# Three mixers and a mixture of experts on one core: the recurrence's projections first, the attention values projected in the rotation steps, the recurrence's output gate computed late and read from PSUM

## What is computed

```python
h = x @ w_cols
h_gla, h_rwkv, h_nsa, h_vres = _split(h, ...)
gq, gk, gv, gg, galr = _split(h_gla, GLA_COLS)
rr, rk, rv, rwlr, ralr, rglr = _split(_token_shift_mix(h_rwkv, rwkv_mu[l]), RWKV_COLS)
o_gla, o_rwkv, o_nsa = _gla_mixer(...), _rwkv7_mixer(...), _nsa_mixer(...)
mix = jnp.concatenate([o_gla, o_rwkv, o_nsa], axis=-1) @ w_out[l]
...
g = (jax.nn.sigmoid(g_lr) @ g2).astype(f32)        # in _rwkv7_mixer
return ((y + bonus) * g).astype(dt)
```

## Time and profile before

| | |
|---|---|
| median of 3 runs | 2021.17 us (2020.33 to 2023.05) |
| profiled execution | 2023.03 us, its span 2021.2 us |
| PE busy | 1966.1 us (97%) |
| DVE, ACT, POOL busy | 855.1, 313.4, 45.1 us |
| mean granted PE clock | 0.993 |
| HBM read | 596.73 MB, mean 296 GB/s |

### The profile page before, as it was taken

One profiled execution on the slowest core, in us unless ns is written; L12 is line 12 of the kernel. 1 busy time (PEld: TensorE's weight loads), 2 busy tenths in 40 slices (PEclk: granted clock), 3 DMA queues, 4 the chain that ended last, 5 costly groups with the idle time before them and its releaser, 6 DMA issues.

```text
span 2021.2 us, 24513 instructions
## 1 busy us (share of the span) xinstructions
PE 1966.1 (97%) x9835; PEld 1115.1 (55%) x9835; DVE 855.1 (42%) x1538; ACT 313.4 (16%) x725; POOL 45.1 (2%) x62
## 2 busy tenths in 40 slices
PE   8999999999999999999999999999999999999997
PEld 7878588748777588749553333333333333333332
DVE  1487588865587586754731111111111111111112
ACT  1335211101435111103410000000000000000001
POOL 0021000000021000000000000000000000000000
PEclk9999999999999999999999999999999999999999
DMA  8540067646630165436298999999999999999996
GB/s 332 217 158 1 32 234 308 251 167 278 263 126 1 41 226 199 171 154 266 89 393 373 428 429 429 427 429 429 427 430 427 430 429 427 429 427 430 429 428 287
DMA packets 44275, 598.75 MB, mean 296 GB/s; under 512 B 5056, under 2 KB 5360, under 8 KB 8464
## 3 DMA queue, kind: packets, MB, share of 16 engines
q1 hardware_dynamic: 44208, 597.82, 71.9%
HBM read 596.73 MB, written 1.07 MB: 296 GB/s over the span
## 4 chain that ended last, share of the span: by engine, by line
PE 82%; DMA 15%; DVE 3%; issue 0%; ACT 0%; SPq 0%; DVEq 0%
PE ps L2349 18%; DMA ring<-in_stream 15%; PE ps L1404 12%; PE ps L2397 8%; PE ps L1489 7%; PE ps L402 6%; PE ps L2323 3%; PE ps L1273 3%; PE ps L361 2%; PE ps L2338 2%; PE ps L419 2%; PE ps L2434 2%; PE ps L1820 1%; PE ps L1986 1%; PE ps L1150 1%; PE ps L1167 1%
## 5 line engine op out<-in xcount | busy, mean ns | idle before, releaser
L2349 PE MATMUL ps<-ring,HT 128*64 128x512 f32 x2176 | 479.4, 594 | 20.0 <-DMA ring<-in_stream 19.2
L2349 PEld LDWEIGHTS ps<-ring,HT 128*64 128x64 f32 x2176 | 152.9, 137 | 340.1 <-issue 289.3
L2397 PE MATMUL ps<-SB,HT 128*64 128x512 f32 x1088 | 249.2, 612 | 0.9 <-ACT HT L2460 0.9
L2505 DVE TENSOR_SCALAR HT<-ps 128x512 f32<-128x512 f32 x34 | 23.5, 692 | 449.8 <-PE ps L2349 449.8
L2397 PEld LDWEIGHTS ps<-SB,HT 128*64 128x64 f32 x1088 | 77.0, 140 | 170.2 <-issue 170.2
L1404 PE MATMUL ps<-ring,SB 128*128 128x256 f32 x704 | 156.0, 379 | 0.3 <-DVE SB L331 0.3
L2454 ACT ACTIVATE HT<-HT 128x512 f32<-128x512 f32 x34 | 21.5, 631 | 843.9 <-DVE HT L2505 843.9
L1404 PEld LDWEIGHTS ps<-ring,SB 128*128 128x128 f32 x704 | 133.6, 190 | 18.8 <-issue 0.7
L2517 DVE TENSOR_TENSOR HT<-ps,TOK 128x512 f32<-128x512 f32 x34 | 23.5, 692 | 281.3 <-PE ps L2397 281.3
L402 PE MATMUL ps<-SB,ring 128*128 128x256 f32 x576 | 126.9, 384 | 1.3 <-DMA ring<-in_stream 1.3
L402 PEld LDWEIGHTS ps<-SB,ring 128*128 128x128 f32 x576 | 110.8, 193 | 17.1 <-issue 1.6
(11 more groups left out here) (489 smaller groups left out, 2251.8 us busy)
## 6 DMA issues: line engine op xcount, KB each, us to landing
ring<-in_stream SPq DMA_DIRECT2D x210, 2048.0 KB, 16.6
SB<-in_stream SPq DMA_DIRECT2D x68, 2048.0 KB, 24.8
SB<-in_ln SPq DMA_DIRECT2D x8, 512.0 KB, 7.0
CST<-in_const SPq DMA_DIRECT2D x1, 1362.0 KB, 5.5
PAR<-in_layer SPq DMA_DIRECT2D x2, 558.5 KB, 11.6
X<-in_x SPq DMA_DIRECT2D x1, 1024.0 KB, 4.9
HN<-in_head_norm SPq DMA_DIRECT2D x2, 512.0 KB, 12.8
SB<-in_cond_row SPq DMA_DIRECT2D x2, 512.0 KB, 10.9
```

Of the source, the lines that this page charges most:

```text
L2349: m = pe.matmul(ps[HD * half:HD * (half + 1), a, :], XE[:, 2 * b + k, q * SLOTS_E:(q + 1) * SLOTS_E], w[:, k, a, half, :], start=False, st ...
L2397: m = pe.matmul(ps[HD * c:HD * (c + 1), 3, :], EHT[:, k, HD * b:HD * (b + 1)], w[:, k, c, :], start=b + k == 0, stop=b + k == 4, skip_grou ...
```

## The change

The columns of the weights are laid out anew: the recurrence's channels are groups 0 to 3 and the first half of 4, GLA's queries and keys follow in 5 and 6, and DVE's `mix_dve` waits for five groups in place of seven. The projections are counted anew: group 11 is now the 24 gate columns of both token halves (`project_gates_pe`), 12 and 13 are GLA's values and gate (`project_tokens_pe`), and group 14 the 256 columns of attention values (`project_values_pe`). The values are projected in the rotation steps 2 and 3 in 16 products, where 13 dummy products go; the slot of their weights is released only there. GLA's gate and the low-rank products come after group 8, not 9. The recurrence's output gate is computed in the second chunk, where three dummy products go, and DVE reads it from PSUM; ACT's copy of it goes. POOL's blocks (`cmp_pool`) move from XT's to LW's and AA's memory and wait for `rw_ops`.

```diff
-T_GQ, T_GK, T_R, T_K, T_V, T_WA, T_G1, T_MISC, T_VC, T_KC, ... = 0, 2, 4, 6, 8, 10, 11, 12, 13, 14, ...
+T_R, T_K, T_V, T_WA, T_G1, T_MISC, T_VC, T_GQ, T_GK, T_KC, ... = 0, 2, 4, 6, 7, 8, 9, 10, 12, 14, ...
...
-                return "proj_ready", 15 * l + [2, 4, 6, 8, 10, 13, 15][s]
+                return "proj_ready", 15 * l + [2, 4, 6, 8, 10, 15, 14][s]
...
+        def project_gates_pe(pe, l):
+            w = slot(AT["in", l, 5]).rearrange("p (k n) -> p k n", k=KT)
+            pe.wait_ge(S("proj_evac"), 15 * l + 8)
+            for t in range(NT):
+                for k in range(KT):
+                    m = pe.matmul(ps[:, proj_bank(11), 24 * t:24 * (t + 1)], XT[:, k, t * P:(t + 1) * P], w[:, k, 384:408],
+                                  start=k == 0, stop=k == KT - 1)
+            m.then_inc(S("proj_ready"), 1)
...
+        def project_values_pe(pe, l, t, ks):
+            w = slot(AT["in", l, 5]).rearrange("p (k n) -> p k n", k=KT)
+            for k in ks:
+                m = pe.matmul(ps[:, proj_bank(14), t * 256:(t + 1) * 256], XT[:, k, t * P:(t + 1) * P], w[:, k, P:P + 256],
+                              start=k == 0, stop=k == KT - 1)
+            if t == NT - 1 and ks[-1] == KT - 1:
+                m.then_inc(S("proj_ready"), 1)
...
         def mix_dve(v, l, I, L):
-            v.wait_ge(S("proj_evac"), 15 * l + 7)
+            v.wait_ge(S("proj_evac"), 15 * l + 5)
...
         def rwkv_ranks_pe(pe, l):
...
-            for t in range(NT):
-                pe.matmul(ps[:, 5, t * T:(t + 1) * T], HT[:, T_G1, t * P:(t + 1) * P], par("g2"), start=True, stop=False)
-                m = pe.matmul(ps[:, 5, t * T:(t + 1) * T], HT[0:32, T_MISC, t * P:(t + 1) * P], par("misc")[0:32, :],
-                              start=False, stop=True)
             m.then_inc(S("rw_z"), 1)
+        def rwkv_gate_high_pe(pe, t):
+            pe.matmul(ps[:, 5, t * T:(t + 1) * T], HT[:, T_G1, t * P:(t + 1) * P], par("g2"), start=True, stop=False)
+        def rwkv_gate_low_pe(pe, t):
+            m = pe.matmul(ps[:, 5, t * T:(t + 1) * T], HT[0:32, T_MISC, t * P:(t + 1) * P], par("misc")[0:32, :],
+                          start=False, stop=True)
+            if t == NT - 1:
+                m.then_inc(S("rw_z"), 1)
...
         def rwkv_gates_act(act, l, I):
-            nc.scalar.activation(GT, ps[:, 5, :].rearrange("p (t c) -> p t c", t=NT), ACT.Copy).then_inc(S("rw_gates"), 1)
+            ins.then_inc(S("rw_gates"), 1)
...
         def chunk_removed_pe(pe, l, j):
                 pe.wait_ge(S("rw_s"), l + 1)
-                clock_pe(pe, 5, 0, 256, 1)
+                rwkv_gate_high_pe(pe, 0)
+                rwkv_gate_low_pe(pe, 0)
...
         def rwkv_norm_dve(v, l, I, L):
-            nc.vector.tensor_tensor(R_XC, R_XC, GT.rearrange("p t c -> p (t c)"), ALU.mult).then_inc(S("head_out"), 1)
+            v.wait_ge(S("rw_z"), 2 * (l + 1))
+            nc.vector.tensor_tensor(R_XC, R_XC, ps[:, 5, :], ALU.mult).then_inc(S("head_out"), 1)
-        N_FL = [view(flat_xt, 1024 + 512 * i, [16, 32]) for i in range(2)]
+        N_FL = [view(SB, 10240 + 512 * i, [16, 32]) for i in range(2)]
...
         def cmp_pool(pool, l):
-            pool.wait_ge(S("proj_ready"), 15 * (l + 1))
+            pool.wait_ge(S("rw_ops"), l + 1)
...
         def mixers_pe(pe, l):
                 if s == GLA_BACK:
-                    clock_pe(pe, 3, 0, 256, 3)
+                    project_values_pe(pe, l, 0, range(4))
...
+                if s == GLA_BACK + 1:
+                    project_values_pe(pe, l, 1, range(4, 8))
...
-                    if part:
+                    if part and j == 0:
                         clock_pe(pe, 5, 0, 256, 1)
+                    elif part:
+                        (rwkv_gate_high_pe, rwkv_gate_low_pe)[part - 1](pe, 1)
...
                 if s == GLA_BACK:
-                    clock_pe(pe, 3, 0, 256, 3)
+                    project_values_pe(pe, l, 0, range(4, 8))
+                    project_values_pe(pe, l, 1, range(2))
                     back_pe(pe, 2 * l, G_XC, 4)
-                    clock_pe(pe, 3, 0, 256, 3)
+                    project_values_pe(pe, l, 1, range(2, 4))
...
                     if u == 1:
-                        clock_pe(pe, 3, 0, 256, 6)
+                        pe.wait_ge(S("proj_evac"), 15 * (l + 1))
+                        clock_pe(pe, 3, 0, 256, 2)
...
         def mixers_act(act, l):
+                if u == 1:
+                    project_act(act, l, (14,))
...
         @block.tensor
-                    project_pe(pe, l, range(5))
+                    project_pe(pe, l, range(9))
...
                 gla_gate_pe(pe, l)
                 rwkv_ranks_pe(pe, l)
-                project_pe(pe, l, (5,))
+                project_pe(pe, l, (9,))
+                project_pe(pe, l, (10,))
                 rwkv_norm_pe(pe, l)
-                project_pe(pe, l, (6,))
+                project_gates_pe(pe, l)
+                project_tokens_pe(pe, l, 0, range(KT))
+                for p in range(2):
+                    rope_pe(pe, l, p)
+                project_tokens_pe(pe, l, 1, range(KT))
                 rwkv_bonus_pe(pe, l)
...
         @block.scalar
                 rwkv_ranks_act(act, l, I)
-                project_act(act, l, (9,))
                 gla_decay_act(act, l, L)
                 rwkv_gates_act(act, l, I)
-                project_act(act, l, (10,))
+                project_act(act, l, (9,))
                 gla_query_act(act, l)
-                project_act(act, l, (11, 12))
+                project_act(act, l, (10, 11))
...
-        cols = np.concatenate([gla[:, 0:512], rw[:, 0:512], rw[:, 512:768], rw[:, 768:896], rw[:, 896:1024], misc,
-                               kv[1], kv[0], kv[2], kv[4], nsa[:, qperm][:, 0:512],
+        cols = np.concatenate([rw[:, 0:512], rw[:, 512:768], rw[:, 768:896], rw[:, 896:1024], misc,
+                               kv[1], gla[:, 0:512], kv[0], kv[2], kv[4], nsa[:, qperm][:, 0:512],
                                kv[3], kv[5], nsa[:, 1280:1304], zero(104), gla[:, 512:1024]], 1)
```

More of the change, by code:

```diff
@@ L363, in proj_bank @@
         def proj_bank(g):
-            return g % 4 if g < 13 else g - 9
+            return g % 4 if g < 12 else (4, 5, 3)[g - 12]
         def project_first_pe(pe, l, t):
@@ L383, in project_first_pe, with project_pe @@
                     m.then_inc(S("proj_ready"), 1)
-        def project_pe(pe, l, slots):
-            def bank_free(g):
-                if g >= 13:
+        def project_pe(pe, l, groups):
+            for g in groups:
+                need_slot(pe, AT["in", l, g // 2])
+                w = slot(AT["in", l, g // 2]).rearrange("p (k n) -> p k n", k=KT)
+                if g >= 4:
+                    pe.wait_ge(S("proj_evac"), 15 * l + g - 3)
+                for j in range(2 if g < 10 else 1):
+                    for k in range(KT):
+                        m = pe.matmul(ps[:, proj_bank(g), j * T:(j + 1) * T],
+                                      w[:, k, (2 * (g % 2) + j) * P:(2 * (g % 2) + j + 1) * P],
+                                      XT[:, k, :], start=k == 0, stop=k == KT - 1)
+                m.then_inc(S("proj_ready"), 1)
@@ L656, in rwkv_gates_act @@
                                                bias=par(bias)[:, c:c + 1])
[L657 to L658 removed]
+                    if c == 0 or b != (4 if l else 7):
+                        I(ins)
+            ins.then_inc(S("rw_gates"), 1)
         def rwkv_square_dve(v, l, I, L):
```

91 lines of the change are left out of this document (39 added, 52 removed).

## The result

| | before | changed |
|---|---|---|
| median of 14 runs, us | 2019.76 (2017.41 to 2023.53) | 2027.70 (2024.49 to 2030.15) |
| ratio, 95% interval | | 1.0040 (1.0032 to 1.0047) |
| profiled execution, us | 2023.03 (span 2021.2) | 2026.21 (span 2024.4) |

The change makes the kernel slower by 7.9 us (0.4%); the interval spans 6.5 to 9.5. The forecast of 2020.5 and its range up to 2025.5 missed it. The page looks as before: PE as busy, the chain as much PE's.

What follows compares the result with a forecast made beforehand. PE's work was taken to bound the projections. Projections -6.2, rotation +2.6 and second chunk +1.3 gave -2.3 us at full clock; +1.6 for the clock made -0.7, so 2020.5 against the median of 2021.17, range 2016.0 to 2025.5.

Steps and rivals of the forecast that it cites:

- I expect one fall there: At layer 1's wait ahead of the low-rank products: the clock drops to half speed once, costing 1.6 us.
- The nearest row: Late in the kernel before: clock at 0.50 from 1455.90 to 1459.10, pricing a drop at 1.6 us.
- The 24-column block is no wait: Gate columns in the projections: claimed to keep full clock, as a row of 64-column products did over 3.62 us.
- The rival that ended on the slow side: Projections: the clock also drops in the 24-column block of both layers and in both waits; +5.7 us (2026.9), chance 0.13.
- Waits at the low-rank products: PE waits for `rw_rank` after group 8 and GLA's gate: 2.04 us in layer 0, 3.47 in layer 1.
- Wait for L674 (now L694) in layer 1: PE waits for DVE ahead of the recurrence's turns in layer 1: 1.0 us.
- The 24-column block: 16 gate-column products, 32 records, bound by their weights: 3.7 us per layer where the 280-column block took 7.55.
- Projections in all: From group 8 to the recurrence's turns: gains of 4.3 us in layer 0 and 1.9 in layer 1, together 6.2.
- Rotation: Value products moved into the rotation steps make `back_pe` later: cost 1.3 us per layer, 2.6 in both, bounds 0 and 2.2.
- Second chunk: Four output-gate halves replace three dummies on PE: cost 0.63 us per layer, 1.3 in both, bounds 0 to 2.5 in both.

Runs made afterwards that it cites:

- the fill: The changed kernel plus 4 (layer 0) and 7 (layer 1) dense dummy products of 256 columns ahead of the low-rank products; +1.7 us against the kernel before.
- the weave: The changed kernel with two gate-column products behind each product of group 10; +4.7 us against the kernel before, -2.2 with dense dummies also in the waits.
- The run with 64 columns: The changed kernel with dense dummies in the waits and 64 columns per gate-column product, the last 24 used; +1.9 us against the kernel before.

## Why the prediction was wrong

**The step that failed is the clock.** It is there twice.

- *"I expect one fall there, at the nearest price, 1.6 us."* The fall came at the place named, behind layer 1's wait, but the size was off: 10.24 us at 0.50, not 3.2. With the fill the segment is 4.05 shorter; with the weave in both, 42.12 - 37.44 = 4.7. The nearest row was a fall behind 0.56 us of idle time; here 3.39 us of it were followed by 4 us of products over 64 and 32 rows that went on at half speed.
- *"The 24-column block is no wait: the row of 64-column products kept 1.00 over 3.62 us."* Wrong as a reason that it keeps the clock, and from one row with more columns. In layer 1 the clock fell at the block in all five profiles that have it in a row. It cost 36.63 - 34.96 = 1.67 in layer 0 and 3.3 in layer 1 (42.06 - 38.76, by the fill with 24 and with 64 columns). The run with 64 columns shows what such a row in one profile is worth: its profile too kept 1.00, while its median, +1.9, is that of 24 columns.

By profiled segments the clock cost 1.67 + (46.11 - 38.76) = 9.0 us, against the 1.6 forecast. The rival that ended on the slow side named this mechanism and gave 2026.9 with a chance of 0.13. It had four falls, 1.6 at each of the two blocks, 3.2 at layer 1's wait and 1.6 at layer 0's, 8.0 in all; the profile had three, of 1.7, 3.3 and about 4, and none at layer 0's wait.

**The rest of the sum held but for the second chunk**, taken from the executions without a fall (34.96 and 38.76):

- *Waits at the low-rank products*: 1.96 and 3.39, forecast 2.04 and 3.47. ACT's rows of layer 1 show the two table loads, one more than in layer 0, that made the difference between the layers:

```profile
524.10 1.28 ACT L644 ACT_TABLE_LOAD   x1
...
525.83 1.28 ACT L645 ACT_TABLE_LOAD   x1
...
527.45 0.40 ACT L646 ACTIVATE HT<-HT 32x256 f32<-32x256 f32 x1
```

- *Wait for L674 (now L694) in layer 1*: 1.10, forecast 1.0.
- *The 24-column block*: at full clock its row is 3.65 long and it holds PE for 3.5 (3.84 in the changed kernel's layer 0, where the clock fell inside it), forecast 3.7; 0.114 us a record by the row. The floor of 25 ns of the Trainium skill ("TensorE: Matmul & The Clock Gate", section "Back-to-back issue gap") would have made it 0.8 (an estimate from that figure); the traces don't bear it out for this shape.
- *Projections in all*: -4.45 and -1.70, forecast -4.3 and -1.9.
- *Rotation*: 1.29 per layer, forecast 1.3.
- *Second chunk*: 2.50 - 1.29 = 1.2 per layer, forecast 0.63, near its upper bound of 1.25. The term took a half by the distance of starts (0.63) but a dummy by the length of its row (0.60). By starts the three dummies of layer 0 held PE for 0.43, 0.53 and 0.43, in all 1.39, and the four halves hold it for 2.32, so 0.93 more; and the first product behind L665 is longer too (0.49, before 0.38):

```profile
213.48 0.60 PE L662 MATMUL ps<-PAR,HT 128*128 128x256 f32 x2
214.01 0.69 PE L665 MATMUL ps<-PAR,HT 32*128 32x256 f32 x2
214.63 0.49 PE L927 MATMUL ps<-SB 128*128 128x128 f32 x2
```

At full clock that is -6.15 + 2.6 + 2.4 = -1.2, the forecast -2.3. With 9.0 for the clock it is the +7.9 of the first table, from the same segments.

**What had been left out** in costing the order: the 280-column block and group 9 were not only work, they were the dense cover of two waits (with group 9 put back the first is gone, and without the 280 columns the second grows to 3.09). The clock was reckoned as an extra of 1.6 to a sum made at full speed. Why the clock fell at just these places, and why only in some executions of layer 0, no run here shows; that dense work in the wait and between the thin products keeps it, they do.

## What to carry to other kernels

Where a change takes dense work away from between thin or waiting stretches, read the granted clock as part of the cost: fill the wait with dense products, or weave the thin products into dense ones, and only then count what was saved. One profile with the clock at 1.00 over a thin row doesn't show that it keeps it; compare several profiles, and look at the mean clock of every run. Moving real work into a wait moves the wait too: ask which result comes later for it, and what stands behind that wait.
